# Conditioning weights of two layers multiplied at other waits of TensorE

## What is computed

```
cond = jax.nn.silu(c)
for i in range(DEPTH_2):
    mod = cond @ ada_w[i] + ada_b[i]
    sh1, sc1, g1, sh2, sc2, g2 = jnp.split(mod, 6, axis=-1)
    h = modulate(rmsnorm(x, norm_g[i, 0]), sh1, sc1)
    ...
    x = x + g1[:, None, :] * y
    h = modulate(rmsnorm(x, norm_g[i, 1]), sh2, sc2)
    ...
    x = x + g2[:, None, :] * y
```

## Time and profile before

| | us |
|---|---|
| median of 3 runs | 2287.05 (2284.98 to 2288.88) |
| profiled execution, from its first to its last instruction | 2286.9 |
| TensorE busy | 1955.4 (86%) |
| DVE busy | 1089.2 (48%) |
| ACT busy | 854.7 (37%) |
| mean granted TensorE clock | 0.950 of full |

### The profile page before, as it was taken

The page is one execution under the profiler, slowest core; times in us unless marked ns, Lnnn a source line. Parts: engine busy times, 40 slices in busy tenths (PEclk is TensorE's granted clock), DMA queues, the critical chain, the costliest instruction groups (busy, mean ns, idle before and its releaser), DMA issues.

```text
span 2286.9 us, 30203 instructions
## 1 busy us (share of the span) xinstructions
PE 1955.4 (86%) x12057; PEld 1401.8 (61%) x12057; DVE 1089.2 (48%) x1666; ACT 854.7 (37%) x1153; POOL 43.3 (2%) x111
## 2 busy tenths in 40 slices
PE   6989997997656566598999998988989998999997
PEld 6968776772111111256899898877665674664672
DVE  3845565432111110223545477875574582674572
ACT  4342345310000000234344357764463462463460
POOL 0010200000000000000000000000000000000000
PEclk9989998998888988899999999999999999999999
DMA  7563561579999999949455544434999999999997
GB/s 261 180 221 111 191 240 70 219 292 392 409 409 409 409 409 409 333 176 371 171 185 185 192 140 144 167 132 144 331 404 384 394 408 409 393 406 409 396 408 285
DMA packets 232012, 663.12 MB, mean 290 GB/s; under 512 B 24580, under 2 KB 33320, under 8 KB 231604
## 3 DMA queue, kind: packets, MB, share of 16 engines
q1 hardware_dynamic: 224108, 652.94, 74.9%
q10 hardware_dynamic: 7752, 8.11, 1.3%
HBM read 659.90 MB, written 1.10 MB: 289 GB/s over the span
## 4 chain that ended last, share of the span: by engine, by line
PE 54%; DMA 22%; DVE 13%; ACT 7%; issue 3%; POOL 0%; ACTq 0%; SPq 0%; DVEq 0%; POOLq 0%
PE psum L263 11%; PE psum L264 11%; PE psum L265 11%; PE psum L252 6%; DMA ring<-in_w_expert_up 5%; DMA ring<-in_w_expert_down 5%; DMA ring<-in_w_expert_gate 5%; PE psum L2485 4%; DMA ring<-in_moe_w_gate 4%; DVE w_lo L202 3%; PE psum L2784 2%; PE psum L2541 2%; ACT w_hi L192 2%; DVE xbc L987 1%; PE psum L1188 1%
## 5 line engine op out<-in xcount | busy, mean ns | idle before, releaser
L202 DVE TENSOR_TENSOR w_lo<-ring,w_hi 128x1024 fp32r<-128x1024 f32 (+1 forms) x498 | 580.6, 1187 | 410.7 <-ACT w_hi L192 403.6
L192 ACT CAST w_hi<-ring 128x1024 fp32r<-128x1024 f32 (+1 forms) x498 | 503.6, 1021 | 395.3 <-PE psum L265 301.3
L2784 PE MATMUL psum<-ring,hT 128*32 128x512 f32 x960 | 148.4, 749 | 115.8 <-DMA ring<-in_w_expert_gate 62.0
L2784 PEld LDWEIGHTS psum<-ring,hT 128*32 128x32 f32 x960 | 30.5, 122 | 226.9 <-issue 87.8
L263 PE MATMUL psum<-w_hi,xg_hi 128*128 128x512 f32 (+1 forms) x384 | 148.2, 386 | 21.1 <-DVE w_lo L202 21.1
L2485 PE MATMUL psum<-ring,xg_pair 128*64 128x512 f32 (+1 forms) x768 | 156.7, 560 | 5.3 <-DMA ring<-in_moe_w_up 5.2
L2388 DVE TENSOR_TENSOR x<-x,psum 128x1024 f32<-128x1024 f32 x26 | 31.2, 1219 | 247.3 <-PE psum L252 247.3
L264 PE MATMUL psum<-w_hi,xg_lo 128*128 128x512 f32 (+1 forms) x384 | 146.2, 381 | 0.0
L265 PE MATMUL psum<-w_lo,xg_hi 128*128 128x512 f32 (+1 forms) x384 | 145.8, 380 | 0.0
L2485 PEld LDWEIGHTS psum<-ring,xg_pair 128*64 128x64 f32 x768 | 54.1, 137 | 102.6 <-issue 99.1
L2806 PE MATMUL psum<-ring,midT 128*32 128x512 f32 x480 | 68.8, 708 | 42.2 <-DMA ring<-in_w_expert_down 42.2
(11 more groups left out here) (697 smaller groups left out, 3674.8 us busy)
## 6 DMA issues: line engine op xcount, KB each, us to landing
ring<-in_moe_w_down SPq DMA_DIRECT2D x176, 512.0 KB, 12.6
ring<-in_w_expert_gate SPq DMA_DIRECT2D x32, 2048.0 KB, 16.9
ring<-in_moe_w_gate SPq DMA_DIRECT2D x128, 512.0 KB, 10.9
ring<-in_moe_w_up SPq DMA_DIRECT2D x128, 512.0 KB, 11.4
ring<-in_w_expert_down SPq DMA_DIRECT2D x30, 2048.0 KB, 18.3
ring<-in_w_expert_up SPq DMA_DIRECT2D x28, 2048.0 KB, 17.6
ring<-in_ada_w SPq DMA_DIRECT2D x24, 2048.0 KB, 11.4
ring<-in_moe_w_gate SPq DMA_DIRECT2D x64, 384.0 KB, 11.8
```

Of the source, the lines that this page charges most:

```text
L192: a.copy(self.buffers(n, src.shape)[0], src).then_inc(*self.hi_made.up())
L202: v.tensor_tensor(lo, src, hi.bitcast(F32), SUB).then_inc(*self.lo_made.up())
L2784: ins = p.matmul(ps[slots_of(j), g * 512:(g + 1) * 512], M.xg[:, 2 * q + k, slots_of(j)], w[:, j, k, :], start=2 * q + k == 0, stop=2 * q ...
```

## The change

Layer 0: pair 3 goes to just ahead of the attention, pair 4 behind it in place of the four constants, pair 5 behind the merge's branch steps in place of the thirteen; NSA's unit 0 goes up into the delta net's tail, in place of pair 3 and ten constants. The ring's order follows: pair 3 ahead of branch (2, 1), pair 4 ahead of branch (1, 0), pair 5 ahead of out0. Layer 1: pairs 1 to 3 stand beside steps 5, 7 and 8 of MLA attention, pair 4 in the norm of the FFN and pair 5 in that of the SSM, both with eight constants in place of 24. `ada_row` holds two pairs. The last gate of layer 1 is added later by DVE ("last_gate"), and the gates' rows are written behind SSM unit b and read back behind unit c.

```diff
@@ order of the units
-    ada_units(0, 3, 4)
     columns_unit(("nsa", 0), w_in, O_Q, 512, row_parts(512))
     columns_unit(("nsa", 1), w_in, O_KV, 512, row_parts(512))
-    ada_units(0, 4, 5)
     columns_unit(("nsa", 2), w_in, O_KV + 512, 256, row_parts(256))
...
     gate_unit(2, 1)
-    ada_units(0, 5, ADA_PAIRS)
+    ada_units(0, 3, 4)
     branch_unit(2, 1)
     gate_unit(1, 0)
     gate_unit(1, 1)
+    ada_units(0, 4, 5)
     branch_unit(1, 0)
     branch_unit(1, 1)
+    ada_units(0, 5, ADA_PAIRS)
...
-        if c == 0:
-            ada_units(1, 1, 2)
-    ada_units(1, 2, ADA_PAIRS)
+    ada_units(1, 1, 4)
     for half in range(2):
         mla_out_unit(half)
+    ada_units(1, 4, 5)
...
+    ada_units(1, 5, ADA_PAIRS)
@@ gdn_pe
-        ada_pe(p, 0, 3)
+        nsa_unit_pe(p, 0)
         ps = banks.take(p, "oT")
-        constant_products(p, ps, ident, 10)
         p.wait_ge(*st.dve.of("o"))
@@ nsa_pe
-        ada_pe(p, 0, 5)
+        ada_pe(p, 0, 3)
...
         attention_pe(p, st, nsa_s, nsa_pT, nsa_jobs, beside=merge_beside_pe)
-        ada_turn_pe(p, 0, 5)
+        ada_turn_pe(p, 0, 3)
+        ada_pe(p, 0, 4)
         ps = banks.take(p, "ynT")
-        constant_products(p, ps, ident, 4)
         p.wait_ge(*st.dve.of("yn"))
@@ merge_pe, proj_pe
             banks.let_go("unit", unit["branch", 1, half])
+            if half == 0:
+                ada_turn_pe(p, 0, 4)
+        ada_pe(p, 0, 5)
...
-        turned_pe(p, st, merged, KD, 13, lambda: finished(p, S["merge"]))
+        turned_pe(p, st, merged, KD, 0, lambda: finished(p, S["merge"]))
+        ada_turn_pe(p, 0, 5)
...
-                constant_products(p, ps, ident, 6)
+                constant_products(p, ps, ident, 5)
@@ mla_beside_pe
         if n == 5:
             heads_pe(p, 3)
+            ada_pe(p, 1, 1)
+        if n == 6:
+            ada_turn_pe(p, 1, 1)
+        if n == 7:
+            ada_pe(p, 1, 2)
+        if n == 8:
+            ada_turn_pe(p, 1, 2)
             ada_pe(p, 1, 3)
...
@@ ffn_pe (ssm_pe: the same with pair 5 and xn_ssm)
-        norm_pe(p, st, xn_ff, 24)
+        ada_pe(p, 1, 4)
+        norm_pe(p, st, xn_ff, 8)
@@ ssm_act
-        a.wait_ge(*st.dve.of("gains"))
-        gates_write_act(a, 1)
...
         ssm_upad_act(a, "b", 0)
-        gates_load_act(a, 1)
+        a.wait_ge(*st.dve.of("last_gate"))
+        gates_write_act(a, 1)
         split.make_hi(a, split.end(c) + PARTS)
         ssm_upad_act(a, "c", 0)
+        gates_load_act(a, 1)
```

More of the change, by code:

```diff
@@ L1196, in ada_act @@
         a.wait_ge(*st.pe.of("ada", layer, n))
-        if n:
-            a.wait_ge(*st.pe.of("ada_turned", layer, n - 1))
-        a.copy(ada_row[:, 0:256], banks.of("ada", layer, n)[:, 0:256]).then_inc(*st.act.up("ada", layer, n))
+        if n >= 2:
+            a.wait_ge(*st.pe.of("ada_turned", layer, n - 2))
+        elif layer:
+            a.wait_ge(*st.pe.of("ada_turned", 0, ADA_PAIRS - 2 + n))
+        a.copy(ada_row[:, 256 * (n % 2):256 * (n % 2) + 256], banks.of("ada", layer, n)[:, 0:256]).then_inc(*st.act.up("ada", layer, n))
         banks.empty(st.act, "ada", layer, n)
@@ L1206, in ada_turn_pe @@
         for f in range(2):
-            ins = product(p, ps[:, 4 * f:4 * f + 4], [(ada_row[:, f * P:(f + 1) * P], ident[:, 0:P:32])])
+            ins = product(p, ps[:, 4 * f:4 * f + 4], [(ada_row[:, 256 * (n % 2) + f * P:256 * (n % 2) + (f + 1) * P], ident[:, 0:P:32])])
         ins.then_inc(*st.pe.up("ada_turned", layer, n))
@@ L1523, in gdn_act @@
         banks.empty(e, "ST")
-        ada_act(a, 0, 3)
+        split.make_hi(a, split.end(unit["nsa", 0]))
     def gdn_dve(v):
@@ L1595, in gdn_dve @@
         banks.empty(d, "WS")
+        split.make_lo(v, split.end(unit["nsa", 0]))
         v.wait_ge(*st.pe.of("AU"))
@@ L1750, in nsa_pool, with nsa_unit_pe @@
         rsqrt_pool(g, st, rc[:, :], 1.0 / 64, "rc")
+    def nsa_unit_pe(p, n):
+        u, w = unit["nsa", n], nsa_units[n][2]
+        ps = banks.take(p, "unit", u)
+        by_token_pe(p, u, h_mix, [[ps[:, t * 512:t * 512 + w] for t in range(NT)]])
     def nsa_pe(p):
@@ L1754, in nsa_pe @@
         e = st.pe
[L1755 to L1761, removed]
+        for n in (1, 2):
+            nsa_unit_pe(p, n)
         p.wait_ge(*st.dve.of("dup"))
@@ L1858, in nsa_act @@
         merge_step_act(a, 2, 3)
-        ada_act(a, 0, 5)
+        ada_act(a, 0, 3)
         attention_act(a, st, nsa_s, nsa_pT, nsa_mx, nsa_den, 1.0, nsa_jobs, beside=merge_beside_act)
+        ada_act(a, 0, 4)
         a.wait_ge(*st.pe.of("ynT"))
@@ L1953, in nsa_dve @@
         attention_dve(v, st, nsa_s, nsa_mx, nsa_den, 1.0, nsa_jobs, nsa_score, nsa_finish, beside=merge_beside_dve)
-        ada_turn_dve(v, 0, 5)
+        ada_turn_dve(v, 0, 3)
         v.wait_ge(*st.act.of("ynT"))
@@ L1973, in merge_act @@
                 merge_step_act(a, 1, 6 * half + n)
+        ada_act(a, 0, 5)
     def merge_rest_dve(v):
@@ L1980, in merge_rest_dve @@
             merge_dve(v, 1, half)
+            if half == 0:
+                ada_turn_dve(v, 0, 4)
     def turned_pe(p, st, src, n_f, idle, begin):
@@ L2025, in proj_dve @@
         turned_dve(v, st, mT, KD)
+        ada_turn_dve(v, 0, 5)
         for half in range(2):
@@ L3011, in modulation_gains_dve @@
         d = st.dve
-        settle(v, v.tensor_tensor(mod[:, :], mod_all[:, 48 * layer:48 * layer + 48], colrange("ada_b_2", 48 * layer, 48 * layer + 48), ADD), d)
+        n = 40 if layer else 48
+        settle(v, v.tensor_tensor(mod[:, 0:n], mod_all[:, 48 * layer:48 * layer + n], colrange("ada_b_2", 48 * layer, 48 * layer + n), ADD), d)
         for s_ in range(2):
@@ L3133, in mla_beside_pe @@
             heads_pe(p, 2)
-            ada_pe(p, 1, 2)
-        if n == 4:
-            ada_turn_pe(p, 1, 2)
         if n == 5:
             heads_pe(p, 3)
+            ada_pe(p, 1, 1)
[5 more added lines that the diff above has]
+            ada_turn_pe(p, 1, 2)
             ada_pe(p, 1, 3)
-        if n == 6:
+        if n == 9:
             ada_turn_pe(p, 1, 3)
[L3142 to L3148, removed]
     def mla_beside_act(a, n):
@@ L3155, in mla_beside_act @@
             heads_act(a, 1)
-            ada_act(a, 1, 1)
         if n == 2:
@@ L3161, in mla_beside_act @@
             heads_act(a, 2)
-            ada_act(a, 1, 2)
         if n == 5:
             heads_act(a, 3)
-            ada_act(a, 1, 3)
+            ada_act(a, 1, 1)
         if n in (7, 8):
-            ada_act(a, 1, n - 3)
+            ada_act(a, 1, n - 5)
         if n == 8:
@@ L3175, in mla_beside_dve @@
             rope_queries_dve(v, 1)
-        if n in (2, 4, 6, 8):
-            ada_turn_dve(v, 1, n // 2)
+        if n in (6, 8):
+            ada_turn_dve(v, 1, n // 2 - 2)
         if n == 9:
-            ada_turn_dve(v, 1, 5)
+            ada_turn_dve(v, 1, 3)
         if n == 9:
@@ L3348, in ffn_pe @@
                 by_feature_pe(p, unit["ff", g, c], h_ff, nf, ready=None if c or g else st.dve.of("h", 4))
+                if c == g == 0:
+                    ada_turn_pe(p, 1, 4)
         pairs = [banks.take(p, "ff_down", half) for half in range(2)]
@@ L3364, in ffn_act @@
         norm_turned_act(a, st, h_ff, modulated_gain(1), modulated_shift(1))
+        ada_act(a, 1, 4)
         for c, nf in enumerate(ff_chunks):
@@ L3398, in ffn_dve @@
             v.tensor_tensor(lo, gated_ff[:, 0:nf * T], hi.bitcast(F32), SUB).then_inc(*d.up("mid", c))
+            if c == 0:
+                ada_turn_dve(v, 1, 4)
         last = unit["ff", 2, len(ff_chunks) - 1]
@@ L3489, in ssm_pe @@
         e = st.pe
-        norm_pe(p, st, xn_ssm, 24)
+        ada_pe(p, 1, 5)
+        norm_pe(p, st, xn_ssm, 8)
         ps = banks.take(p, "dt")
@@ L3499, in ssm_pe @@
         by_feature_pe(p, unit["ssm", "b", 0], h_ssm, ready=st.dve.of("h", 4))
+        ada_turn_pe(p, 1, 5)
         p.wait_ge(*st.dve.of("da"))
@@ L3646, in ssm_act @@
         norm_rows_act(a, st, xn_ssm, ss_ssm)
-        a.wait_ge(*st.dve.of("gains"))
-        gates_write_act(a, 1)
         norm_turned_act(a, st, h_ssm, modulated_gain(0), modulated_shift(0))
+        ada_act(a, 1, 5)
         softplus_exp_act(a, st, sp, "sp")
@@ L3824, in ssm_dve @@
         split.make_lo(v, split.end(b) + PARTS)
+        ada_turn_dve(v, 1, 5)
+        v.wait_ge(*S["ada"].dve.last())
+        v.tensor_tensor(mod[:, 40:48], mod_all[:, 88:96], colrange("ada_b_2", 88, 96), ADD).then_inc(*d.up("last_gate"))
         v.wait_ge(*st.pe.of("daT"))
```

7 lines of the change are left out of this document (removed).

## The result

The changed kernel takes 2299.3 us (median of 17 runs, 2292.1 to 2304.4), the kernel before 2288.9 in the same series: ratio **1.0043, 95% interval 1.0035 to 1.0051**, slower by 0.43%. A second series on another occasion gave 1.0028 (1.0019 to 1.0037). So the change costs some 6 to 10 us. An execution's time is 1.7 to 1.9 us above its span; the profiled execution of the changed kernel has a span of 2299.9 and a time of 2301.76.

What follows compares the result with a forecast made beforehand. TensorE was taken to bound the chain (54%), with DVE, ACT or loads ending some waits. Terms -3.5 + 11.1 - 8.0 + 0.5 + 1.0 = +1.1 on 2286.9 gave 2288.0 us, range 2278.5 to 2295.

Steps and rivals of the forecast that it cites:

- Delta net's tail: Delta net's tail to NSA's unit 1: starts 5.8 us earlier, slow clock costs 2.3; net -3.5 (-5.8 to -2.2).
- Attention's end and out0: NSA attention's end: pair 4 and out0's late load delay DVE's merges 9.1 us, slow clock 2.0; net +11.1.
- Rival 1: NSA attention's end: out0 lands before its first low half is wanted, only 2.5 us lost; total 2279.5; chance 0.25.
- MLA: MLA attention: five pairs beside it become three, saving TensorE time and waits; -8.0 us (-10.9 to -5).
- Rival 2: MLA attention: DVE's kcat, not TensorE, sets the pace, so only -3 us; total 2293; chance 0.15.
- FFN: FFN norm: a pair and eight constants replace 24 constants at equal length; turn between TensorE's units costs +0.5 us.
- Rival 3: FFN and SSM norms: the clock falls in both waits, +2.3 us each; total 2292.6; chance 0.10.
- SSM: SSM norm and gates: ACT may stand at the rows' read behind unit c; 0 to 4, taken as +1.0 us.

Runs made afterwards that it cites:

- e5: The changed kernel with 20 constants ahead of NSA's unit 1, in the bare wait behind the delta net's transposes; 2303.2 us, ratio 1.0074 to the kernel before.
- e4: The changed kernel with DVE's two merges, and the turn between them, ahead of the low halves of out0's first three parts; ratio 1.0002 to the kernel before.
- e8: The kernel before with only DVE's two merges put ahead of the low halves of out0's first three parts; ratio 1.0007 to the kernel before.
- e1: The changed kernel with layer 1's gates read back at head 5 of the SSM's head loop; 2293.5 us, ratio 1.0022 to the kernel before.
- e2: The kernel before with only the change's layer 1 edits and both halves of ada_row; ratio 0.9992 to the kernel before.
- e3: The kernel before with only the change's layer 0 edits and both halves of ada_row; ratio 1.0051 to the kernel before.
- e9: The kernel before with only the change's layer 1 edits, the gates read back at head 5; 2283.0 us, ratio 0.9975 to the kernel before.

## Why the prediction was wrong

By its steps:

- **Delta net's tail**, -3.5: -4.2 and -3.7. Right, with its parts. The wait was put at 5.4 and is 5.57; the slow clock was put at 2.3, and e5 gives back 1.7 to 2.2 when the clock is held. The sentence on the Trainium skill's section Terms of "TensorE: Matmul & The Clock Gate" would have made it 3.6; e5 and the rows of the trace speak for the smaller number.
- **Attention's end and out0**, +11.1: +11.2 (2.6 + 8.6) and +12.3. Right in mechanism and size. The load took 17.8, where 17.6 was reckoned; ACT waited for it, the merges behind it, and the transposes ran in the slow clock. e4 shows by one edit on DVE that it is this order, and e8 that the order alone is nothing. Rival 1, that the queue does not bite, is out.
- **MLA**, -8.0: -6.9 and -6.7. Mis-sized by about 1. I counted the wait of 1.66 at the last pair as gone "as that load comes earlier"; it is still there, since that pair moved up as much as its load:

```profile
1080.01 3.66 PE L1188 MATMUL psum<-ring,cond 128*32 128x256 f32 x64 [1.65 <-DMA ring<-in_ada_w]
```

  Rival 2, that kcat sets the pace, is out too: the gain arrived in the changed kernel, e1 and e2.
- **FFN**, +0.5: +0.4 and +0.3. Rival 3, 2.3 for the clock in each norm's wait, is out: it is not in these entries, nor in the +0.9 of the SSM in e1.
- **SSM**, "0 to 4, I take +1.0": **+6.8 and +7.1. This is the step that failed.** The prediction named the right instruction ("ACT reads the rows back behind unit c and may have to stand there") and had a row for the load behind such a write, 19.3, but it put no length on the write itself: it bounded the wait by 4 without a row and took a quarter of that. The trace of the kernel before holds no landing of the writes. In the changed kernel the later one, issued at 1355.2, lands 16.2 after that, at 1371.4, and unit c's copy is done at 1366.1: a wait of 5.3 before the read is issued. In e3, whose layer 1 is that of the kernel before, the later write took 10.9, which would have cost ACT nothing; there the load beside it is issued 1.5 behind the writes, in the changed kernel 0.3 ahead of them. So the row that was missing is the length of the write beside the load that it meets now. What was late next were ACT's work for the heads and the decays, all of it behind that read. e1 settles it.
- **Base.** The sum stood on the span of 2286.9, as if that were the execution's time; executions take 1.7 to 1.9 more, and the kernel before has a median of 2288.9 over 17 runs. This shifts the time that was named by 2, not the change.

With +6.8 in place of +1.0 the sum would have been +6.9, where the two series give +9.8 and +6.4 by their ratios; the first has some 3 more that no stage names. The forecast of no change rested on a gain and a loss of the same size, -8.0 and +7.6; in such a sum each small term decides the sign, and one of the small ones had no row.

## What to carry to other kernels

A load moved later in a queue is priced at its first consumer on every engine, not only at TensorE: in the kernel before TensorE wanted out0 at 447 and DVE, which prepares it ahead of other work, from 431 on the earlier trace rows. Work that waits for no load belongs ahead of work that may. And a round trip through HBM that hid behind 24 us of other work is a dependence like any other: when its start moves, it needs a length of its own, which changes with the load that it now runs beside, and the read is best put where its data are used.

## What the runs showed of the hardware

The same instructions run in the full or in the slow clock from one execution to the next, far from any change. The window from 125 to 130 us lies ahead of all that differs between these kernels: before, the changed kernel, e1 (columns as above):

```profile
125.00:130.00 5.00, 5.00 (x57) 2.47 (x50) 0.00 (x0) 1.82 (x4) 0.41 (x3) 0.94 0.18 32
```

```profile
125.00:130.00 5.00, 5.00 (x52) 2.26 (x52) 0.00 (x0) 0.17 (x1) 0.10 (x1) 0.50 0.01 3
```

```profile
125.00:130.00 5.00, 5.00 (x40) 2.35 (x33) 0.00 (x0) 3.14 (x5) 0.00 (x0) 1.00 0.40 112
```

The granted clock is 0.94, 0.50 and 1.00, and what follows at 131.8 stands 3.0 later than before in the changed kernel and 1.3 earlier in e1. Likewise at the end of MLA attention: from 1078 to 1090 the clock is 1.00 in e2 and 0.64 in e9, whose instructions up to there are the same, and MLA's entries differ by 4.7. So one profiled execution decides on a term of 2 to 4 us only where the term repeats in others.

The second point is the write of the gates: two transfers of 4 KB took 12.8 and 16.2 us to land, and the load of 2 MB beside them took 13.3 where it had taken 7.9 without such a write. It repeats in all eleven traces with this order: the later write takes 15.9 to 17.2, the load 13.0 to 14.5.
